# Embedding gate done one row tile at a time, six down units held by tile at the third feed-forward layer, five weight units in places of their own

## The reference, cut to what matters

```
x = x + 0.5 * swiglu(rmsnorm(x, ffn2_norm), ffn2_wgu, ffn2_wdown)      # "f1"
e = rmsnorm(p @ ple_proj, ple_norm)                                     # embedding
gate = sigmoid(rmsnorm(x, ple_gate_norm) @ ple_gate_w)                  # "gate"
x = x + gate * e
# second block
h = rmsnorm_2(x, g_pre[0]) * (1 + sc1) + sh1
x = x + 0.5 * gt1 * rmsnorm_2(swiglu_2(h, w_gu1, w_dn1), g_post[0])     # "f2"
h = rmsnorm_2(x, g_pre[1]) * (1 + sc2) + sh2                            # "mix2" begins
y = token_mixer(h, ...)
```

## Time and profile before

| | us |
|---|---|
| median of 3 runs | 1323.79 (1323.59 to 1324.05) |
| the profiled execution's own time | 1323.46 |
| its span in the trace | 1321.7 |
| PE busy in the span | 1309.8 (99%) |
| DVE, ACT, POOL busy | 947.1, 745.5, 67.5 |

### The profile page before, as it was taken

The page is one execution under the profiler, slowest core; times in us unless marked ns, Lnnn a source line. Parts: engine busy times, 40 slices in busy tenths (PEclk is TensorE's granted clock), DMA queues, the critical chain, the costliest instruction groups (busy, mean ns, idle before and its releaser), DMA issues.

```text
span 1321.7 us, 17177 instructions
## 1 busy us (share of the span) xinstructions
PE 1309.8 (99%) x6391; PEld 1094.5 (83%) x6391; DVE 947.1 (72%) x1352; ACT 745.5 (56%) x1150; POOL 67.5 (5%) x132
## 2 busy tenths in 40 slices
PE   9999999999999999999999999999999999999998
PEld 6888888888888888888788888889988888888886
DVE  6788877856666778797777887677876456766554
ACT  6454458567874544546754435866457664745452
POOL 3100100000000000010000000100000000000000
PEclk9999999999999999999999999999999999999999
DMA  9999966543375699894589996656553356377762
GB/s 289 315 300 310 318 221 191 164 123 106 90 257 178 203 293 301 298 350 158 167 248 301 298 305 215 202 169 177 167 153 112 112 166 216 123 215 218 221 198 101
DMA packets 185491, 282.45 MB, mean 214 GB/s; under 512 B 20386, under 2 KB 133258, under 8 KB 185408
## 3 DMA queue, kind: packets, MB, share of 16 engines
q1 hardware_dynamic: 172672, 238.22, 58.1%
q0 software_dynamic: 12576, 43.06, 9.7%
q10 hardware_dynamic: 160, 0.07, 0.0%
HBM read 268.66 MB, written 1.05 MB: 204 GB/s over the span
## 4 chain that ended last, share of the span: by engine, by line
PE 94%; DVE 3%; ACT 2%; issue 0%; DMA 0%; SPq 0%; DVEq 0%; POOL 0%; ACTq 0%
PE ps L2116 25%; PE ps L2077 16%; PE ps L2079 16%; PE ps L2078 16%; PE ps L2305 2%; PE ps L2091 1%; PE ps L2092 1%; PE ps L2093 1%; PE ps L2131 1%; PE ps L2201 1%; PE ps L2202 1%; PE ps L2203 1%; DVE w_lo L1228 1%; PE ps L2226 1%; PE ps L2380 1%; PE ps L2364 1%
## 5 line engine op out<-in xcount | busy, mean ns | idle before, releaser
L1228 DVE TENSOR_TENSOR w_lo<-raw,w_hi 128x1024 fp32r<-128x1024 f32 (+2 forms) x431 | 513.7, 1212 | 202.8 <-ACT w_hi L704 201.0
L704 ACT ACTIVATE w_hi<-raw 128x1024 fp32r<-128x1024 f32 (+2 forms) x431 | 448.4, 1054 | 349.5 <-DMA raw<-in_ffn_wgu_dram 102.9
L2077 PE MATMUL ps<-w_hi,a_hi 128*128 128x512 f32 (+1 forms) x968 | 383.4, 396 | 0.7 <-DVE w_lo L1228 0.4
L2079 PE MATMUL ps<-w_hi,a_lo 128*128 128x512 f32 (+1 forms) x968 | 375.6, 388 | 0.0
L2078 PE MATMUL ps<-w_lo,a_hi 128*128 128x512 f32 (+1 forms) x968 | 375.0, 387 | 0.0
L2079 PEld LDWEIGHTS ps<-w_hi,a_lo 128*128 128x128 f32 x968 | 181.7, 188 | 38.0
L2077 PEld LDWEIGHTS ps<-w_hi,a_hi 128*128 128x128 f32 x968 | 182.0, 188 | 36.5 <-DVE w_lo L1228 0.8
L2078 PEld LDWEIGHTS ps<-w_lo,a_hi 128*128 128x128 f32 x968 | 182.1, 188 | 35.2
L2116 PE MATMUL ps<-w_hi,hid_hi 128*128 128x512 f32 x300 | 93.1, 392 | 0.0
L2116 PE MATMUL ps<-w_hi,hid_lo 128*128 128x512 f32 x300 | 92.4, 389 | 0.0
L2116 PE MATMUL ps<-w_lo,hid_hi 128*128 128x512 f32 x300 | 92.4, 389 | 0.0
(11 more groups left out here) (439 smaller groups left out, 1609.4 us busy)
## 6 DMA issues: line engine op xcount, KB each, us to landing
raw<-in_ffn_wgu_dram SPq DMA_DIRECT2D x176, 256.0 KB, 4.6
raw<-in_w_in_dram SPq DMA_DIRECT2D x88, 512.0 KB, 3.7
raw<-in_w_gu_dram SPq DMA_DIRECT2D x176, 256.0 KB, 3.7
ada<-in_w_ada_dram POOLq DMA_DIRECT2D x72, 512.0 KB, 6.1
raw<-in_ffn_wdown_dram SPq DMA_DIRECT2D x44, 512.0 KB, 5.7
raw<-in_w_dn_dram SPq DMA_DIRECT2D x44, 512.0 KB, 4.4
raw<-in_w_in_dram SPq DMA_DIRECT2D x36, 256.0 KB, 3.1
raw<-in_w_out_dram SPq DMA_DIRECT2D x16, 512.0 KB, 4.8
```

What stands on the lines that cost most here:

```text
L704: act.activation(room(u, w_hi, w_hi2)[:, 0:nk * n], room(u, raw, raw2)[:, 0:nk * n], ACT.Copy).then_inc(hi_ready, 1)
L1228: dve.tensor_tensor(room(u, w_lo, w_lo2)[:, 0:nk * n], room(u, raw, raw2)[:, 0:nk * n], room(u, w_hi, w_hi2)[:, 0:nk * n].bitcast(F32), AL ...
L2077: pe.matmul(dst(t)[:, 0:n], a[0], slot(u, w_hi, kk, n), start=kc == 0, stop=False)
L2079: i = pe.matmul(dst(t)[:, 0:n], a[1], slot(u, w_hi, kk, n), start=False, stop=kc == KC - 1)
```

## The change

It touches three things.

**Gate.** PE multiplies all 8 gate units for tile 0, then all 8 for tile 1, and before the last two of tile 1 it turns tile 0 for f2. Tile 1 of the result goes to the banks that held the embedding product, so PE waits for tile 1's `emb` first. ACT takes the embedding's squares before it converts gate units 4 to 7, and DVE makes both pairs of inverse roots in one sequence on a 2x2 block, also before it converts units 4 to 7. Tile 0's gated sum, norm and turn follow while PE does tile 1. The six fillers go.

**Third layer.** The first six up units (four of the first block, two of the second) are done for tile 0, with tile 1's turn before the sixth, and then for tile 1. At the down end the last six units are held: tile 0 takes units 16 and 17, the sum of the modulation rows, and units 18 to 21 half by half; tile 1 takes 16 to 19 and then 20 and 21 half by half. The four fillers go.

**Places.** Gate units 2 and 3 lie where rows of `hid_hi` and `hid_lo` were, down units 19, 20 and 21 where `ada`, `acc_m` and `brow` were. SP therefore waits for `gate_lo` before it loads down unit 19, and everything later in its queue waits with it.

```
+        own = {u_pg + 2: 0, u_pg + 3: 1}
+        own.update({u_wo2 + k: 2 + k for k in range(EXTRA)})
+        HELD = 6
+        own.update({ffn[2][1] + FC - 3 + k: 2 + EXTRA + k for k in range(3)})
...
+        at_own = [ARENA + 8 * S * 4, HR0 + 8 * S * 4] + [QA0 + 8 * D * k for k in range(EXTRA)] + [ADA0 + 8 * D * k for k in range(3)]
...
 SyncE, load_unit(u)
+                if u == u_pg + 2:
+                    sp.wait_ge(used, ffn[1][1] + 18)
+                if u == ffn[2][1] + FC - 3:
+                    sp.wait_ge(sem("gate_lo"), 3)
...
 ScalarE, ffn_part(f)
-                w.to(dn + 18)
+                if f != 2:
+                    w.to(dn + 18)
                 hidden_hi(f, HGROUPS - 1)
-                w.to(dn + FC + (1 if f == 2 else 2))
+                w.to(dn + FC + 2)
...
 ScalarE, gate
-            w.to(u_pg + 6)
+            act.wait_ge(used, u_pp + 2)
             for t in range(T):
                 act.activation(emb[:, t, :], wide(t), ACT.Square, accum_out=pss[:, t:t + 1])
+            w.to(u_pg + 6)
...
             w.to(u_pg + KC + 2)
+            tile_hi("f2", 0)
             act.wait_ge(used, u_pg + KC)
-            act.activation(h[:, 1, :], behind(1), ACT.Sigmoid, scale=rstd[:, 1:2])
-            tile_hi("f2", 0)
+            for n in range(2):
+                c = slice(512 * n, 512 * (n + 1))
+                act.activation(h[:, 1, c], acc(1, n), ACT.Sigmoid, scale=rstd[:, 1:2])
             load_table(ACT.Sqrt)
+            w.to(u_pg + KC + 3)
             norm_tile("f2", 1)
             norm_root("f2", 1)
             load_table(ACT.Silu)
+            w.to(u_pg + KC + 4)
             tile_hi("f2", 1)
...
 VectorE, gate
+            dve.wait_ge(sem("pss_ready"), 2)
+            rsqrt(sums[:, 1:4:2, 0:2], sums[:, 0:4:2, 0:2], ...)
             w.to(u_pg + 6)
-            dve.wait_ge(sem("pss_ready"), 2)
-            rsqrt(prs[:, :], pss[:, :], 1.0 / D, small(rt))
-            for t in range(T):
+            for t in (1, 0):
                 dve.scalar_tensor_tensor(emb[:, t, :], wide(t), prs[:, t:t + 1], grow[:, :], ...)
...
+            gate_sum(0)
+            w.to(u_pg + KC - 1)
...
             scaled_turn("f2", factor)
+            w.to(u_pg + KC + 2)
             chunk_lo("f2", 0, 0)
             chunk_lo("f2", 0, 1)
+            tile_lo("f2", 0, 2)
+            gate_sum(1)
+            w.to(u_pg + KC + 3)
             tile_root("f2", 1)
             normalise("f2", 1)
+            w.to(u_pg + KC + 4)
             chunk_lo("f2", 1, 0)
...
 TensorE
-                for k in range(FC - SKEW):
+                for k in range(FC - HELD if f == 2 else FC - SKEW):
...
+            def held_rows(dn):
+                for t in range(T):
+                    k0 = FC - SKEW if t == 0 else FC - 2
+                    for k in range(FC - HELD, k0):
...
+                        i = row_half(dn + k, k, t, FC - 1, hid_hi, hid_lo, 0)
+                    if t == 0:
+                        sum_mods("f2", UPB + 1)
+                    for half in range(2):
+                        for k in range(k0, FC):
...
+                            i = row_quarter(dn + k, k, t, half, FC - 1, hid_hi, hid_lo)
...
-            first_rows(u_pg, "gate", None, KC, a_hi, a_lo, bank=4, all_of=True)
-            last_rows(u_pg, KC, a_hi, a_lo, bank=4)
-            pe.wait_ge(sem("emb_ready"), T)
-            busy(6, 0)
-            pe.wait_ge(sem("gate_ready"), T + 1)
-            turn_tile("f2", h, 0)
+            for k in range(KC):
+                pe.wait_ge(lo_ready, u_pg + k + 1)
+                i = row_half(u_pg + k, k, 0, KC - 1, a_hi, a_lo, 4)
+            i.then_inc(sem("first_tile"), 1)
+            pe.wait_ge(sem("emb_ready"), 1)
+            for k in range(KC):
+                tile_ready("gate", 1, k)
+                if k == KC - 2:
+                    turn_tile("f2", h, 0)
+                row_half(u_pg + k, k, 1, KC - 1, a_hi, a_lo, 0).then_inc(used, 1)
             ffn_part(2)
             pe.wait_ge(sem("mod_taken"), 9)
-            busy(4, 7)
             turn_tile("mix2", h, 0)
```

More of the change, by code:

```diff
@@ L174, in two_blocks @@
         wa2 = keep("wa2", [16, 512])
[L175 to L178, removed]
+        sums = keep("sums", [P, 4, 8])
+        ss, rstd, pss, prs = (sums[:, k, 0:2] for k in range(4))
         rt = keep("rt", [P, 3, 36])
@@ L398, in two_blocks @@
         EXTRA = 6
[L399 to L400 removed]
+        own = {u_pg + 2: 0, u_pg + 3: 1}
+        own.update({u_wo2 + k: 2 + k for k in range(EXTRA)})
+        HELD = 6
+        own.update({ffn[2][1] + FC - 3 + k: 2 + EXTRA + k for k in range(3)})
+        home, freed_by, last_user, turn_of = [], [], [None] * RING, 0
         for u in range(NU):
[L402 to L403 removed]
+            if u in own:
+                home.append(None)
                 freed_by.append(None)
             else:
[L406 removed]
+                r = turn_of % RING
+                turn_of += 1
                 home.append(r)
@@ L409, in two_blocks @@
                 last_user[r] = u
[L411 to L414, removed]
+        raw_own, lo_own, hi_own = [], [], []
+        at_own = [ARENA + 8 * S * 4, HR0 + 8 * S * 4] + [QA0 + 8 * D * k for k in range(EXTRA)] + [ADA0 + 8 * D * k for k in range(3)]
+        for k, base in enumerate(at_own):
+            raw_own.append(place(f"raw_own{k}", [P, UNIT], F32, base)[0])
+            v, _, e = place(f"lo_own{k}", [P, UNIT], F32R, base)
+            lo_own.append(v)
+            v, _, e = place(f"hi_own{k}", [P, UNIT], F32R, e)
+            hi_own.append(v)
+            assert e <= HB
         def room(u, ring, extra):
-            return extra[:, u - u_wo2] if u in held else ring[:, home[u]]
+            return extra[own[u]] if u in own else ring[:, home[u]]
         count = [0] * (RING + EXTRA // 2)
@@ L421, in two_blocks @@
         for u in range(NU):
-            which = RING + (u - u_wo2) // 2 if u in held else home[u]
+            if u in own:
+                k = own[u]
+                which = RING + (k if k < 2 else (k - 2) // 2 if k < 2 + EXTRA else k - 2 - EXTRA)
+            else:
+                which = home[u]
             count[which] += 16 * len(units[u][0])
-            need.append(32 if u in held else count[which])
+            need.append(count[which])
             land_at.append(which)
+        for k in range(0, EXTRA, 2):
+            need[u_wo2 + k] = need[u_wo2 + k + 1]
         landed = [sem(f"raw_landed{r}") for r in range(RING + EXTRA // 2)]
@@ L1428, in folded_tiles @@
                 tile_lo(key, 1)
-                row_scales(key)
+                if key != "gate":
+                    row_scales(key)
             def turned_lo(key, hi=a_hi, lo=a_lo, units_between=False, cs=range(KC)):
@@ L2132, in row_quarter @@
                 return i
-            def last_halves(u0, n, hi, lo):
-                for t in range(T):
-                    for half in range(2):
-                        for k in range(n - SKEW, n):
-                            if t == 0 and half == 0:
-                                pe.wait_ge(lo_ready, u0 + k + 1)
-                            i = row_quarter(u0 + k, k, t, half, n - 1, hi, lo)
-                            if t == 1 and half == 1:
-                                i.then_inc(used, 1)
-                        if t == 0 or half == 0:
-                            i.then_inc(sem("first_tile"), 1)
             def last_rows(u0, n, hi, lo, bank=0, late=None, halves=False):
@@ L2256, in ffn_part @@
                     if j == 0 and f > 0:
-                        first_cols(up, acc, FFN[f], x if f == 1 else h, (0, 2, 3, 5)[f], 6 if f == 3 else 4)
+                        first_cols(up, acc, FFN[f], x if f == 1 else h, 2 if f == 1 else 5, 4 if f == 1 else 6)
                         continue
-                    for i in range(2 if f == 3 and j == 1 else 0, 4):
+                    for i in range(2 if f >= 2 and j == 1 else 0, 4):
                         if f == 0 and j == 0 and i in (1, 2):
```

68 lines of the change are left out of this document (37 added, 31 removed).

## The result

The changed kernel takes 1329.17 us (median of 6 runs, 1327.12 to 1329.97); the kernel before took 1323.69 beside it (6 runs). The ratio is 1.0035, 95% interval 1.0024 to 1.0046: slower by more than 0.2%. A later series of the same kernel gave 1329.66 and 1.0042 (1.0030 to 1.0054). The forecast was 1327.5, range 1322.0 to 1330.5, slower with a chance of 0.62.

The account below looks back on a forecast made before the run. PE, busy 99% of the span, was taken as the bound. Gate +0.5, down-unit waits +4.0 and the end −0.5 sum to +4.0 on the profiled 1323.46, with the runs' median 0.3 higher: 1327.5, range 1322.0 to 1330.5.

Parts of the forecast that it names:

- The gate, +0.5: Gate to second block of up columns: new waits lose 4.1 us instead of 3.6, so 0.5 slower.
- The first wait: At the gate, PE waits 0.6 us for DVE's conversion of gate unit 4.
- The second: Tile 0's turn for f2 waits 2.0 us: its squares stand behind up unit 2's conversion, which waits for its load.
- The third: After tile 1's turn, PE waits 1.5 us for the conversion of the sixth up unit.
- are lost now: PE's 3.6 us of fillers and waits at the gate before the change, the most the gate part can bring.
- The fourth wait: At down units 19 to 21, loaded only after m_lo, PE waits 2.4, 0.85 and 0.7 us, 4.0 in all.
- The end's give-back: Last down product to mix2's first: 2.55 us instead of 3.07, so 0.5 faster.
- The clock: Rival: PE's clock falls to half at two waits, 1.65 us lost each, 1330.8; chance 0.05.
- the row of 3.3 us: Profile of before, last stretch: PE idle 5.7 us, with 3.3 us at full clock and the rest at half.
- a case with two falls: The clock rival's time, 1330.8, with 1.65 us lost at each of two waits; the range ends at 1330.5.
- Small waits: Rival: down-unit waits at their low end, +2.15 − 0.5, gate even; +1.6, 1325.1; chance 0.25.
- the faster rival: Rival: conversions at up unit 2 and down unit 19 never last at PE; −3.6 − 0.5, 1319.4; chance 0.13.

Follow-up runs that it names:

- e1: Changed kernel with the old down end, its ring places and four fillers, so only the gate's part is changed; 1323.96 us, ratio 1.0003.
- e4: Changed kernel with SP's wait before the last three down units moved from m_lo to the last modulation product; 1325.43 us, ratio 1.0010.
- e13: Changed kernel run again unaltered, for the spread of its executions; 1329.66 us, ratio 1.0042.
- e3: Changed kernel with ACT's squares of tile 0 at the gate ahead of up unit 2's conversion; 1326.11 us, ratio 1.0022.
- e2: Changed kernel with the gate's pieces undone, so only the down end's part is changed; 1327.50 us, ratio 1.0028.
- e6: Changed kernel with up units 4 and 5 converted ahead of tile 1's sigmoids on ACT and its root on DVE; 1327.73 us, ratio 1.0029.
- e5: Changed kernel with nine filler products on PE ahead of tile 0's turn for f2; 1327.67 us, ratio 1.0024.
- e7: Changed kernel with the last hidden piece back behind the conversions of down units 17 and 18; 1327.22 us, ratio 1.0021.
- e9: Changed kernel with the edits of e3, e4 and e6 together; 1322.29 us, ratio 0.9989.
- e12: Changed kernel with the last three down units in the ring, without SP's wait for m_lo; 1333.04 us, ratio 1.0067.
- e11: e9 with DVE's conversions of up units 4 and 5 moved ahead of tile 1's gated sum; 1321.55 us, ratio 0.9980.
- e10: Kernel before the change, without its six fillers at the gate ahead of the turn for f2; 1323.97 us, ratio 1.0001.

## Why the prediction came out as it did

**The gate, +0.5: right.** Where the clock did not fall there, the gate stretch grew by 0.72 (e1), 0.52 (e4) and 0.45 (e13). The first wait was forecast at 0.6 and came to 0.43. The second was forecast at 2.0 and came to 2.28, by the chain that was named (e3); the load took 4.28 from issue to conversion, for 3.78. The third was forecast at 1.5 and came to 1.2, and tile 1's own chain was hidden behind it as forecast. Of the 3.6 us that "are lost now" some 3.2 went: e1's waits come to 3.9, and its stretch is 0.72 longer.

**The fourth wait, 4.0: right in sum and order.** 2.4, 0.85 and 0.7 were forecast (the prediction's own terms give 2.3, 0.8 and 0.8), and 2.5, 0.6 and 0.8 came. m_lo was 1.29 later against the down units, for 1.25, and by the way that was named: the piece could start when its gather had landed, 39.5 behind the first down product, for 39.35. The load took 3.6 from issue to conversion, for 3.5 to its landing. From one execution to the next this moves: m_lo is 0.5 later than before in e2 and 1.85 later in e6, and the wait 3.1 and 4.4. The Trainium skill, "DMA: Bandwidth & Descriptors", section "Anatomy of one DMA — SWDGE (gpsimd) path", gave an estimate of 3.2 for the load and 3.1 for the wait; here the row of before was the better guide, and the measurement decides.

**The end's give-back, −0.5: right in kind, a little more in size.** mix2 starts 2.4 behind the last down product, where 2.55 was forecast and 3.07 stood before: −0.7. The down stretch of e4, which has no fourth wait, is shorter by the same 0.7.

**The clock, chance 0.05: the step that failed.** "My longest wait, 2.4, is shorter than that" carried the small chance: the row of 3.3 us showed that a clock falls in a long standstill, not that a shorter one is safe. It fell behind 2.13 in the changed kernel and behind 1.83 in e5. The price of a fall was right, 1.65 against 1.7 at the gate; the chance was not, since by their mean clock nine executions of twelve had one, somewhere, and the prediction's sum has none. So 1327.5 is what the three executions without a fall nearly take (1327.1), and the median lies a fall higher. That it still lies inside the range is in part luck: the upper end was set just short of a case with two falls, and by their times most executions had one. The Trainium skill, "TensorE: Matmul & The Clock Gate", section "HAM oscillation — how this bites in real kernels", spoke for this rival. The traces of after, e3, e5, e7 and e13 agree with it (0.50 granted behind a wait), though the waits of its example are longer than theirs.

**Small waits, 0.25, and the faster rival, 0.13.** Neither came. The second would have needed tile 0's squares ahead of the conversion that waits (e3) and a load that isn't tied to m_lo (e4). With both (e9) the two stretches are 2.4 shorter than before, where that rival had 4.1; the first wait and 0.7 on tile 1's rows are among what is left.

## What to carry to other kernels

A place of its own for a unit is worth what the wait ahead of its load costs: tie the load to the last reader of the bytes that it overwrites, and let the later step wait for the rest (e4: 3.9 us of wait gone). An in-order engine that waits for a load holds back what stands behind it, so put the short work on the critical chain ahead of such a wait (e3, and e12 for the reverse). When work moves forward to end one wait, look at what now stands behind that work (e6: two conversions held tile 1's rows back by 1.3). And price a wait on PE of about 2 us with a possible fall of the clock beside it, 1.7 here.

## What the runs showed of the chip

The same standstill was followed by a half clock in one execution and not in another. The table has, for each profile, PE's idle time ahead of the gate's turn, the longest one at the last three down units, and where the granted clock was 0.50 ahead of the last product.

| profile | at the gate's turn | at the down units | half clock |
|---|---|---|---|
| after | 2.13 | 2.35 | 3.4 us at the gate |
| e1 | 2.17 | none | none |
| e2 | 0.3 | 1.55 | none |
| e3 | none | 2.23 | 3.4 us at the down units |
| e4 | 1.97 | none | none |
| e5 | filled | 1.83 | 6.8 us at the down units |
| e6 | 2.24 | 2.72 | none |
| e7 | 1.97 | 0.46 | 3.4 us at the gate |
| e9, e11 | none | 0.2 or less | none |
| e10 | 1.59 | none | 3.4 us at 403.8, behind 2.00 at another layer |
| e12 | 1.95 | none, 7.51 at mix2's turn | 6.8 us from within the 7.51 |
| e13 | 1.95 | 2.90 | 3.4 us at the down units; 3.4 us at 404.2, behind 2.10 at another layer |

No profile has a fall behind a single wait of 1.6 or less. At the gate two of the seven profiles with a standstill of 1.95 to 2.24 have one. What decides between two executions is open, and the falls at 404 have nothing to do with the change.
